# Fewer, fuller input tiles in the mixer of a two-layer streaming encoder, and one top-k selection at a later place

## The reference, cut to what matters

```python
u = rmsnorm(x, P['mix_pre_gain'][l])
(q_lat, kv_lat, k_r, q_b, k_b, v_b, q_c, k_c, v_c, q_i, k_i, w_i,
 g_a, g_b, g_c) = jnp.split(u @ P['w_in'][l], IN_OFFSETS, axis=-1)
...
k_rope = rope(k_r, q_pos)          # 32 columns, one rotated key for all 8 heads
```

## Time and profile before

| | |
|---|---|
| median of three runs | 3212.32 us |
| profiled execution | 3217.1 us, span 3215.3 us |
| TensorE matmul busy | 3045.0 us, 95% of the span |
| VectorE / ScalarE / GpSimd busy | 47% / 31% / 33% |
| mean granted TensorE clock | 0.98 |

### The profile page before, as it was taken

One profiled execution on the slowest core, in us unless ns is written; L12 is line 12 of the kernel. 1 busy time (PEld: TensorE's weight loads), 2 busy tenths in 40 slices (PEclk: granted clock), 3 DMA queues, 4 the chain that ended last, 5 costly groups with the idle time before them and its releaser, 6 DMA issues. The chain is left out here.

```text
span 3215.3 us, 53586 instructions
## 1 busy us (share of the span) xinstructions
PE 3045.0 (95%) x22902; PEld 2817.9 (88%) x22902; DVE 1521.5 (47%) x1645; ACT 1009.8 (31%) x1615; POOL 1069.8 (33%) x499
## 2 busy tenths in 40 slices
PE   8999979999999989999899999799999999899997
PEld 7999977966878989999899999779567789899997
DVE  4554241763345446553265542328623554555523
ACT  3222223353445232222232222333634452322221
POOL 3344323312232424434334434223022324243432
PEclk9999989999999999999999999899999999999998
DMA  6221232111111222222212222322121113122221
GB/s 179 79 91 68 90 111 96 60 55 57 50 57 57 89 94 81 89 83 73 106 66 83 87 73 98 101 80 76 40 67 50 63 54 116 66 92 78 79 82 64
DMA packets 43099, 255.44 MB, mean 79 GB/s; under 512 B 6048, under 2 KB 6144, under 8 KB 26048
## 3 DMA queue, kind: packets, MB, share of 16 engines
q1 hardware_dynamic: 37008, 235.64, 21.0%
q0 software_dynamic: 5840, 17.50, 2.0%
q10 hardware_dynamic: 96, 0.08, 0.0%
HBM read 237.34 MB, written 15.85 MB: 79 GB/s over the span
## 5 line engine op out<-in xcount | busy, mean ns | idle before, releaser
L419 POOL TENSOR_TENSOR ring_r<-ring,piece_h 128x1024 fp32r<-128x1024 f32 (+1 forms) x240 | 630.2, 2627 | 1025.8 <-ACT piece_h L1108 1025.8
L419 POOL TENSOR_TENSOR ring_r<-ring,piece_m 128x1024 fp32r<-128x1024 f32 (+1 forms) x172 | 369.1, 2151 | 866.4 <-ACT piece_m L1108 866.1
L1108 ACT ACTIVATE piece_h<-ring 128x1024 fp32r<-128x1024 f32 (+1 forms) x240 | 274.9, 1147 | 1151.2 <-PE PS L620 1142.5
L615 PE MATMUL PS<-uT_r,piece_h 128*128 128x272 f32 x2688 | 555.9, 288 | 6.1 <-DVE sq L1512 6.1
L615 PE MATMUL PS<-u_l,piece_h 128*128 128x272 f32 x2688 | 556.3, 288 | 0.0
L620 PE MATMUL PS<-uT_r,ring_r 128*128 128x272 f32 x3328 | 451.1, 288 | 0.0
L620 PEld LDWEIGHTS PS<-uT_r,ring_r 128*128 128x128 f32 x3328 | 430.0, 188 | 0.0
L615 PEld LDWEIGHTS PS<-uT_r,piece_h 128*128 128x128 f32 x2688 | 420.9, 188 | 7.0 <-ACT piece_h L1108 7.0
L615 PEld LDWEIGHTS PS<-u_l,piece_h 128*128 128x128 f32 x2688 | 421.1, 188 | 0.0
L615 PE MATMUL PS<-act_l,piece_h 128*128 128x272 f32 x1408 | 292.4, 290 | 0.0
L615 PE MATMUL PS<-act_h,piece_h 128*128 128x272 f32 x1408 | 291.7, 288 | 0.0
(11 more groups left out here) (235 smaller groups left out, 4637.0 us busy)
## 6 DMA issues: line engine op xcount, KB each, us to landing
ring<-in_w_up SPq DMA_DIRECT2D x88, 1024.0 KB, 4.8
ring<-in_w_dn SPq DMA_DIRECT2D x64, 704.0 KB, 4.1
ring<-in_w_mg SPq DMA_DIRECT2D x48, 768.0 KB, 4.4
ring<-in_w_in SPq DMA_DIRECT2D x24, 1024.0 KB, 4.8
ring<-in_w_out SPq DMA_DIRECT2D x8, 1024.0 KB, 4.9
x_spill<-xT SPq DMA_DIRECT2D x2, 2176.0 KB, 8.7
xT<-x_spill SPq DMA_DIRECT2D x2, 2176.0 KB, 8.5
ring<-in_w_vb SPq DMA_DIRECT2D x4, 1024.0 KB, 4.8
```

Of the source, the lines that this page charges most:

```text
L419: nc.gpsimd.tensor_tensor(ring_r[:, ch[0] % NSLOT, at:at + n], w, hi, ALU.subtract).then_inc(S["w_low"], 1)
L615: mm(PS[:, 2 * u + b, 0:HALF], w, x[k][:, HALF * b:HALF * b + HALF], start=first and k == 0 and n == 0, stop=False)
L1108: A(buf[:, hs, 0:n], ring[:, ch % NSLOT, at:at + n], ACT.Copy).then_inc(S["w_high"], 1)
```

## The change

- `kI` and `kC` become one tile `kk`, third in the order, with `k_i` in PSUM rows 0 to 63 and `k_c` in rows 64 to 127. ScalarE writes both keys to both halves of the partitions: 12 copies. `qI0` and `qI1` now come first.
- `kr` and `krs` are no more products with `w_in`. The 32 columns of `k_r` lie in the unused part of `vw` (rows 64 to 95), and two small float32 matmuls for each of the two tiles, with constant matrices `cst[64:96, 6]` and `[7]`, copy them four times, once straight and once swapped.
- `v0`/`v1` weights come in four chunks of 1024 columns, each released by its own product's end; `vw` shares a chunk with `qI3`. Input pieces fall from 30 to 27 per layer. A `pad` tile without work keeps the count even.
- `select` of the sample rows moves from before branch B to after the rotation of the queries.
- GpSimd's DMAs of the keys' rows move with the tiles. `kr_raw` lies elsewhere, since `vw_f` is now read late.

```diff
@@ -99,11 +100,11 @@
 
 def mixer_tiles():
 
-    t = ["kI"] + [f"qI{i}" for i in range(4)] + ["kC", "vw", "v0", "v1"]
+    t = ["qI0", "qI1", "kk", "qI2", "qI3", "vw", "v0", "v1"]
     t += [f"qC{i}" for i in range(4)] + ["kr", "krs"] + [f"ql{i}" for i in range(KQ)] + [f"kv{i}" for i in range(KKV)]
     t += [f"qB{i}" for i in range(4)] + [f"kB{i}" for i in range(4)]
     t += [f"uq{i}" for i in range(4)] + ["qr0", "qs0", "qr1", "qs1"]
-    t += [f"kA{i}" for i in range(4)] + [f"vA{i}" for i in range(4)]
     return t + [f"wo{n}" for n in range(KD)]
...
+V_CHUNKS = 4
+LATE_TILES = TILES[8:12] + TILES[14:27]
 MIX_CHUNKS = ([("w_in", i, 2048, TILES[2 * i + 1]) for i in range(3)]
-              + [("w_vw", 0, 1024, "vw"), ("w_vb", 0, 2048, "v1"), ("w_vb", 1, 2048, "v1")]
-              + [("w_in", 3 + i, 2048 if i < 9 else 1024, TILES[min(10 + 2 * i, 27)]) for i in range(10)]
+              + [("w_vb", i, 1024, f"V{i}" if i + 1 < V_CHUNKS else "v1") for i in range(V_CHUNKS)]
+              + [("w_in", 3 + i, 2048 if i < 8 else 1024, LATE_TILES[min(2 * i + 1, 16)]) for i in range(9)]
               + [("w_uq", 0, 1536, "uq3"), ("w_uq", 1, 1536, "qs1"), ("w_ukn", 0, 1024, "kA3"), ("w_ukv", 0, 1024, "vA3")]
               + [("w_mg", 3 * n + b, 1536, m) for m, (b, n) in enumerate(MERGES)]
               + [("w_out", i, 2048, f"wo{2 * i + 1}") for i in range(4)])
 assert len(MIX_CHUNKS) == CH_MIX
 
-IN_PIECES = ([(i // 2, (i % 2) * 1024, 1024) for i in range(6)]
-             + [(3, 0, 1024)] + [(4 + i // 2, (i % 2) * 1024, 1024) for i in range(4)]
-             + [(6 + i // 2, (i % 2) * 1024, 1024) for i in range(19)])
+IN_PIECES = ([(i // 2, (i % 2) * 1024, 1024) for i in range(6)] + [(3 + i, 0, 1024) for i in range(V_CHUNKS)]
+             + [(7 + i // 2, (i % 2) * 1024, 1024) for i in range(17)])
+assert len(IN_PIECES) == N_IN
 
 OUT_PIECES = [(44 + i // 2, (i % 2) * 1024, 1024) for i in range(KD)]
 
-PIECE_OF = {t: i for i, t in enumerate(TILES[:7])} | {t: 11 + i for i, t in enumerate(TILES[9:28])} | {f"wo{n}": 78 + n for n in range(KD)}
+PIECE_OF = {t: i for i, t in enumerate(TILES[:6])} | {t: 10 + i for i, t in enumerate(LATE_TILES)} | {f"wo{n}": N_IN + 48 + n for n in range(KD)}
...
 VA_KEYS = [(0, 1), (2, 3), (4, 5), (6,)]
...
-        kr_raw = region(22296, 2, TOK)
+        kr_raw = region(20184, 2, TOK)
...
                     by = MIX_CHUNKS[k][3]
-                    if by in TILE:
+                    if by in V_DONE:
+                        sp.wait_ge(S["v_step"], l * 3 + V_DONE[by])
+                    elif by in TILE:
...
-                lows(2, 4)
-                evacuated("kI")
+                lows(2, 5)
+                evacuated("kk")
                 row("p_ki", kI[0:DH, 0:SEQ], "rows_ki")
                 row("s_ki", kI[0:DH, KEY_NEW:NKEY], "rows_ki")
-                lows(4, 13)
+                lows(5, 12)
                 evacuated("v0")
                 evacuated("v1")
-                evacuated("kC")
...
-                lows(13, 30)
+                lows(12, N_IN)
                 pool.wait_ge(S["rope_step"], l * 3 + 3)
...
-                    tile_span(l, f"qC{p // 4}", u_h, u_lo, IN_PIECES[11 + p // 4], 12 * (p % 4), 12 * (p % 4) + 12)
-                for i in range(15, 30):
-                    name = TILES[9 + i - 11]
-                    split_tile(name, u_h, u_lo, IN_PIECES[i][0], IN_PIECES[i][1])
+                    tile_span(l, f"qC{p // 4}", u_h, u_lo, IN_PIECES[10 + p // 4], 12 * (p % 4), 12 * (p % 4) + 12)
+                for i, name in enumerate(("kr", "krs")):
+                    tile(name, [(cst[64:96, 6 + i, :], vw_f[64:96, 0:TOK])])
+                for name in LATE_TILES[4:]:
+                    split_tile(name, u_h, u_lo, *IN_PIECES[PIECE_OF[name]][:2])
...
                 for name in ("vA2", "vA3"):
                     pe.wait_ge(vacated[TILE[name] % 2], l * T_LAYER + turn_of(name) + 3)
+                alone(pe)
+                pe.sem_inc(done[TILE["pad"] % 2], 1)
+                pe.sem_inc(vacated[TILE["pad"] % 2], 1)
                 pe.wait_ge(S["qr_ready"], l * 2 + 2)
                 attend(l, 0)
...
 
-                for i in range(4):
-                    to_blocks(f"qI{i}", qI[:, i, :])
-                to_keys("kC", kC)
+                to_blocks("qI0", qI[:, 0, :])
+                to_blocks("qI1", qI[:, 1, :])
+                u = evac("kk")
+                for r, dst in ((0, kI), (DH, kC)):
+                    for e in range(2):
+                        to = dst[DH * e:DH * e + DH]
+                        A(to[:, 0:HALF], PS[r:r + DH, 2 * u, 0:HALF], ACT.Copy)
+                        A(to[:, HALF:SEQ], PS[r:r + DH, 2 * u + 1, 0:SEQ - HALF], ACT.Copy)
+                        ins = A(to[:, KEY_NEW:NKEY], PS[r:r + DH, 2 * u + 1, SEQ - HALF:HALF], ACT.Copy)
+                ins.then_inc(vacated[u], 1)
+                to_blocks("qI2", qI[:, 2, :])
+                to_blocks("qI3", qI[:, 3, :])
                 to_blocks("vw", vw_f)
...
                                                in1=rstd_kv[:, c:c + b - a], op0=ALU.mult, op1=ALU.mult).then_inc(S["lat_ready"], 1)
-                select(l, 4, 3)
                 dve.wait_ge(S["rows_ki"], 16 * (l * 2 + 2))
                 branch_b(l)
+                select_last(l, 3, 3)
                 dve.wait_ge(S["rows_out"], 16 * (l * 12 + 12))
...
                         dve.wait_ge(vacated[TILE[name] % 2], l * T_LAYER + turn_of(name) + 3)
                     V.tensor_tensor(qAr[:, g, :], qAr[:, g, :], rope_t, ALU.add).then_inc(S["qr_ready"], 1)
                     dve.wait_ge(S["qr_ready"], l * 2 + g + 1)
+                select(l, 4, 4)
                 attend(l, 0)
                 attend(l, 1)
...
+    m = np.arange(P)
+    cst[64 + m % ROPE, 6, m] = 1
+    cst[64 + (m + ROPE // 2) % ROPE, 7, m] = 1
...
-    krs = part["kr"][swap]
-    cols = np.concatenate([part["ki"], part["ki"], part["qi"], part["kc"], part["kc"], part["qc"],
-                           part["kr"], part["kr"], part["kr"], part["kr"], krs, krs, krs, krs, part["ql"], part["kv"],
-                           part["qb"], part["kb"], part["kv"][:128]])
+    none = np.full(P, at[-1])
+    cols = np.concatenate([part["qi"][:256], part["ki"], part["kc"], part["qi"][256:], part["vc"], part["kr"], part["wi"], none[:24],
+                           part["qc"], part["ql"], part["kv"], part["qb"], part["kb"], none])
     w_in = a["w_in"].reshape(L, KD, P, -1)
+    w_in = np.concatenate([w_in, np.zeros((L, KD, P, 1), np.float32)], axis=3)
```

More of the change, by code:

```diff
@@ L70 @@
 PC_FFN = 2 * KF + 2 * KD
-PC_MIX = 30 + 48 + 8
+N_IN = 27
+PC_MIX = N_IN + 48 + 8
 PC_A, PC_M, PC_B = 0, PC_FFN, PC_FFN + PC_MIX
@@ L105, in mixer_tiles @@
     t += [f"uq{i}" for i in range(4)] + ["qr0", "qs0", "qr1", "qs1"]
-    t += [f"kA{i}" for i in range(4)] + [f"vA{i}" for i in range(4)]
+    t += [f"kA{i}" for i in range(4)] + [f"vA{i}" for i in range(4)] + ["pad"]
     return t + [f"wo{n}" for n in range(KD)]
@@ L155, in build @@
         ring_r = nc.alloc_sbuf_tensor_at("ring_r", [P, NSLOT, SLOT], F32R, offset=ring_at)
-        cst = sb("cst", [P, 6, P])
+        cst = sb("cst", [P, 8, P])
         ropes = sb("ropes", [P, 2, TOK])
@@ L497, in gate_low @@
                 def gate_low(m):
-                    low(l, PC_M, 30 + 2 * m, (CH_M + 20 + m, 0), 0, 1024)
+                    low(l, PC_M, N_IN + 2 * m, (CH_M + 20 + m, 0), 0, 1024)
                 def branch_low(m):
-                    low(l, PC_M, 31 + 2 * m, (CH_M + 20 + m, 1), 1024, 512)
+                    low(l, PC_M, N_IN + 1 + 2 * m, (CH_M + 20 + m, 1), 1024, 512)
                 pool.wait_ge(S["sb_out"], l * 5 + 5)
@@ L534, in _ @@
                 for n, (ch, at, m) in enumerate(OUT_PIECES):
-                    low(l, PC_M, 78 + n, (CH_M + ch, n % 2), at, m)
+                    low(l, PC_M, N_IN + 48 + n, (CH_M + ch, n % 2), at, m)
                 ffn(l, PC_B, CH_B)
@@ L699, in split_tile @@
                     open_tile(l, t % 2, T_M + t // 2)
-                    split_product(l, t % 2, l * PC_LAYER + PC_M + piece, piece % 2, ring_r[:, (ch + chunk_of) % NSLOT, at:at + 1024],
+                    split_product(l, t % 2, l * PC_LAYER + PC_M + piece, (piece if piece < N_IN else piece - N_IN) % 2, ring_r[:, (ch + chunk_of) % NSLOT, at:at + 1024],
                                   x_h, x_l)
@@ L706, in mixer @@
                            piece_m)
-                for i in range(2, 7):
+                for i in range(2, 6):
                     split_tile(TILES[i], u_h, u_lo, IN_PIECES[i][0], IN_PIECES[i][1])
@@ L719, in mixer @@
                 for i in range(4):
-                    piece = 7 + i
+                    piece = 6 + i
                     slot, at, _ = IN_PIECES[piece]
@@ L765, in mixer @@
                     at = (i % 4) * KQ * P
-                    tile(TILES[28 + i], [(w[:, at + k * P:at + k * P + P], ql[:, k, :]) for k in range(KQ)])
```

(21 more changed lines are left out.)

11 lines of the change are left out of this document (5 added, 6 removed).

## The result

| | before | after | ratio, 95% interval |
|---|---|---|---|
| median of the runs on one chip | 3213.49 us (3211.82 to 3215.07) | 3184.02 us (3181.74 to 3185.0) | 0.9908 [0.9892, 0.9923] |
| profiled execution | 3217.1 us, span 3215.3 | 3185.0 us, span 3183.2 | |

The kernel is 29.5 us faster between the medians and 32.1 us between the two profiled executions; 30.6 were forecast.

The account below looks back on a forecast made before the run. TensorE, busy 95% of the span, was taken as the bound. Per layer 18.12 us saved less 2.8 for the pair gives 15.3, for two 30.6: from 3212.3 to 3181.7 us (0.9905), range 3175 to 3191.

Parts of the forecast that it names:

- Three tiles of 6.04 us: TensorE, per layer: `kr`, `krs` and one early tile (`kC` merged with `kI`) go, saving 18.12 us.
- The pair, 2.8 us: TensorE after `qC3`: small matmuls for `kr` and `krs`, with a wait between, cost 2.8 us per layer.
- The bounds, 1.3 to 3.7: Cost of `kr` and `krs`: 1.3 us without wait at 64-row speed, 3.7 if each waits for high part and copy.
- rival 2: Clock falls at the new wait between `kr` and `krs`: 5.4 us for two layers, 3187 us; chance 12%.
- The changes of mode: Four tiling-mode switches around `kr` and `krs` cost 0.4 us per layer; 0.1 us was put into the sum.
- `kk` on ScalarE, GpSimd, SyncE, pad: nothing: Twelve copies of `kk` (2.44 us), new waits and DMAs are covered and cost nothing; `pad` under 0.1 us.
- Branch B is ready: At branch B's earlier start VectorE's norm ends at 648.3, `kB3` at 663.2: 15 us of slack.
- It would just have fitted: Selection left before branch B would end at 664.3, 1 us behind `kB3`; VectorE's first work there comes 3.4 us after `kB3`.
- Rival 1: VectorE takes back the saved tail, so only `kC` counts: 12.1 us saved, 3200 us; chance 4%.
- The selection's new place: After the rotation, before attention: 15.97 us of selection hidden in VectorE's 23.23 us wait, 7.2 left; cost nothing.
- Rival 3: Selection, its VectorE operations blocked by GpSimd, holds up attention and the kernel gets slower: 3257 us; chance 2%.
- rival 4: Tiles go but time doesn't: a weight chunk or unit comes late after each moved tile; 3208 to 3215 us; 3%.

Follow-up runs that it names:

- interleaved version: Changed kernel with `kr` inside `qC2` and `krs` inside `qC3`, each behind 64-row index scores: 3182.76 us, 0.9893; a second one, also over 128 rows: 3179.01 us, 0.989.
- the two kernels with spacers: Changed kernel with 48 or 24 matmuls of 272 columns, whose sums nobody reads, after those of `kk`: 3197.48 us (0.9949) with 48, 3195.35 us with 24.

## Why the prediction came out right

It named TensorE as the bound and counted its matmuls, and 30.6 us against 29.5 (medians) and 32.1 (profiled executions) bears that out. Inside it two terms were mis-sized, in opposite directions.

1. *Three tiles of 6.04 us.* Right for the two late ones: the interleaved version's stage is shorter by 12.08 us to the hundredth. The early tile is worth 7.5 us. It went together with the half clock at the first 512-column matmuls, which took 1.5 us of each layer. The prediction had this stretch among its rows, as the price of a rival at another place, and did not ask whether the change would end it. A first stage with half clock stands in all four layers of the kernels with `kI` and `kC` (before, and before with the selection moved) and in none of the 20 layers of kernels with `kk` and nothing put in; in the two kernels with spacers, in one layer of four. So its going is shown to come with the merge; the mechanism isn't shown.

2. *The pair, 2.8 us.* Without half clock 3.03 us: 86.86 - (95.91 - 12.08). The wait is 0.55 us, not 0.8, and each of the two lasts 1.11 us to the next start and not 0.91; over 128 rows it is 0.82 us. The bounds, 1.3 to 3.7, held. To this comes half clock, 1.5 us, in 12 of the 14 layers in which the pair lies as in the change: rival 2's mechanism, given 12%, does happen. Its price was near (1.8 forecast), and its argument against, the shorter wait, was wrong. Filling the wait, or 128 rows with the wait kept, left no half clock in two layers each, and the two interleaved versions had none at the pair in four. That the wait and the few rows are both needed is one reading. It isn't shown: each edit was seen in one execution, each also shifts what follows by some tenths of a us, and the spacers show that a shift upstream, there of 3 us, can matter by itself.

So the fourth stage gave 7.55 us and not 9.28, and the first 7.5 and not 6.04: 15.05 per layer for 15.3. The total was right partly because 1.5 us fell away at one place and came at another. The one error, a clock that was taken to stay as it was where the work around it changes, was made twice.

3. *The changes of mode.* The prediction counted four around `kr` and `krs`. The two stand next to each other in the change, so there are two: from 128 rows to 32 and back. Over 128 rows there are none, and the stage is 0.18 us shorter although the wait is 0.19 longer. In the interleaved version `kr` and `krs` each follow a 64-row matmul, so 128 rows save one change each, two in all; there the saving is 0.36 us (129.36 to 129.00). The Trainium skill (TensorEngine Tiling (Array Packing), Tiling Modes) has a change of mode drain TensorE; the sign agrees. With the longer wait counted in, both places give some 0.2 us for each change that goes, so the 0.1 us that the sum took from one row was low. But what 32 rows cost by themselves is in this too: no run separates the number of rows from the change of mode.

4. *`kk` on ScalarE, GpSimd, SyncE, pad: nothing.* Right. The copies took 2.95 us (2.44 forecast), TensorE's unit was free at 481.6, and the next start was 2.13 us off. The third and fifth stage moved by under 0.3 us outside of half clock.

5. *Branch B is ready.* Right, with more slack than forecast: the norm ended at 638.65, 19.1 us before `kB3` (15 forecast), and VectorE waited 21.90 us. The 3.63 us of waiting for ScalarE's root in the earlier trace rows went, as forecast; the norm's last four operations also took 2.10 us, not the 3.8 from 648.14 to 651.96. "It would just have fitted" was right in the sign and too tight: 7.24 us were left. Rival 1 is out.

6. *The selection's new place.* Right: hidden, 9.23 us left (7.2 forecast, the selection taking 14.2 us and not 15.97), worth nothing in either direction (0.9904 and 0.9908 without and with it, 0.9997 alone). The threefold selection shows the edge where it was put: past the cover each us is paid. Rival 3's mechanism is real, but it acted in the old place and not in the new one (last section), and rival 4 is out by the beat of 6.04 us.

## What to carry to other kernels

Where one engine is busy 95% of the span, count its instructions and read the beat of the engine that it releases; the rest of a change has to be shown hidden, wait by wait. Then look at every stretch of lower clock near the change: an edit can end one or begin one without touching the wait that it follows, at 1.5 us each here, and only a stage-by-stage table over several executions tells this from the edit's own price. A small matmul in a gap was better placed between other products here, and over all 128 rows.

## What the runs showed of the hardware

- The same wait of 2.06 us before 512-column matmuls was followed by half clock (0.57 granted, starts 0.42 us apart) or by full clock (0.23 apart) in kernels that differ in TensorE's work before it. With 24 matmuls put in, half clock followed in the first layer of one execution and full clock in the second. A wait of 0.55 us between 32-row matmuls was followed by half clock in 12 of 14 layers, one of 0.74 us between 128-row matmuls in neither of two.
- From execution to execution of one kernel these stretches come and go (third and fourth stage of the changed kernel: 43.57 or 45.03, 86.86 or 88.36), and they come in steps of about 1.5 us (1.45 to 1.7). The Trainium skill (TensorE: Matmul & The Clock Gate, Part 1) says that the number of matmuls at the low clock varies between runs of one kernel; these traces agree.
- Two float32 matmuls of 272 columns between other products held TensorE 1.11 us over 32 rows and 0.82 over 128, the changes of mode included. Fewer rows are not dearer as such: the pair of 64-row index scores in the earlier trace rows, of 256 columns, took 0.63.
- One operation of the selection waited for GpSimd in the old place. VectorE before the change, and GpSimd at that time:

```profile
662.03 2.14 DVE L1639 TENSOR_SCALAR xT<-xT,m 128x288 f32<-128x288 f32 x1
```

```profile
661.60 2.40 POOL L419 TENSOR_TENSOR ring_r<-ring,piece_m 128x1024 fp32r<-128x1024 f32 x1 [3.64 <-ACT piece_m L1108]
```

  It ends at 664.17, just after GpSimd's low part at 664.00. In the second layer it reads the same (2.14 us, its end at 2257.73 and GpSimd's at 2257.56). With the selection back in its old place in the changed kernel the operation starts later under the low part and takes 0.72 us, and again ends just behind it (648.57 and 648.41). With GpSimd idle in the new place the same operation, at 765.48, takes 0.37 us. That is the 1.8 us by which the selection became shorter.
